# Input norm of each layer as plain transposes with the inverse roots multiplied in afterwards, and the last expert's products reordered around the combine

## The reference

```python
def layer(x):                                   # x: 512 x 1024
    h = x * rsqrt(mean(x * x, -1) + 1e-6) * norm1_g
    p = h @ w_in                                # 1024 -> 2304, split among three mixers
    x = x + concat(hgrn2(p), attention(p), s5(p)) @ w_out
    h = x * rsqrt(mean(x * x, -1) + 1e-6) * norm2_g
    # top 1 of 4 expert groups, top 2 of its 8 experts, for each token
    y_e = (silu(h_e @ w_gate[e]) * (h_e @ w_up[e])) @ w_down[e]     # 32 experts, FF 512
    return x + sum(gate[t, e] * y_e[t])
```

## Time and profile before

| | |
|---|---|
| three runs, median (lowest to highest) | 1594.12 us (1593.08 to 1594.84) |
| the profiled execution: its time, its span | 1589.54 us, 1587.6 us |
| PE busy, share of the span | 1534.9 us, 97% |
| DVE, ACT, POOL busy | 620.1, 428.6, 375.5 us |
| moved by transfers | 470.01 MB, 296 GB/s on average |
| opening of layer 0: PE's first group product | at 15.49 us |
| opening of layer 1: PE's first group product | at 801.70 us |
| PE's last product | starts 1577.4 us |

### The profile page before, as it was taken

How to read it: one execution, slowest core, us unless ns; L and a number is a source line. 1 busy time by engine, 2 the same in 40 slices (tenths; PEclk the granted TensorE clock), 3 DMA queues, 4 the chain that set the end, 5 groups by cost and what they waited for, 6 DMA issues and landing times.

```text
span 1587.6 us, 20334 instructions
## 1 busy us (share of the span) xinstructions
PE 1534.9 (97%) x8214; PEld 794.5 (50%) x8214; DVE 620.1 (39%) x1236; ACT 428.6 (27%) x766; POOL 375.5 (24%) x440
## 2 busy tenths in 40 slices
PE   8999999999999999998899999999999999999986
PEld 5655566555444444443357546655554444444432
DVE  1688546462122212311327965474622122123114
ACT  3664641211111111111235647403111111111102
POOL 5571880000000000000264637700000000000003
PEclk9999999999999999999999999999999999999999
DMA  9300403959999999999860003059699999999997
GB/s 394 144 0 14 146 2 85 419 219 420 429 427 426 428 426 427 428 426 427 339 272 1 0 28 134 1 165 417 236 426 427 425 427 427 426 427 428 425 427 297
DMA packets 57969, 470.01 MB, mean 296 GB/s; under 512 B 19417, under 2 KB 19545, under 8 KB 30194
## 3 DMA queue, kind: packets, MB, share of 16 engines
q1 hardware_dynamic: 50626, 452.37, 68.8%
q0 software_dynamic: 7104, 16.24, 2.8%
q10 hardware_dynamic: 144, 0.07, 0.0%
HBM read 447.69 MB, written 26.74 MB: 299 GB/s over the span
## 4 chain that ended last, share of the span: by engine, by line
PE 84%; DMA 11%; ACT 2%; DVE 2%; issue 1%; POOL 0%; POOLq 0%; SPq 0%; ACTq 0%; DVEq 0%
PE bank L1006 23%; PE bank L647 13%; PE bank L1043 11%; PE bank L996 9%; PE bank L778 7%; DMA hbuf<-wu 7%; DMA ring<-wd 4%; PE bank L641 2%; PE bank L709 2%; PE bank L722 2%; PE bank L739 2%; PE bank L983 1%; PE bank L1030 1%; PE bank L618 1%; PE bank L635 1%; PE bank L855 1%
## 5 line engine op out<-in xcount | busy, mean ns | idle before, releaser
L2225 POOL DMA_INDIRECT expert_rows<-raw_qd,store_rows x60 | 58.7, 979 | 1005.6 <-ACT raw_qd L1431 850.7
L1006 PE MATMUL bank<-ring,hbuf 128*64 128x512 f32 x640 | 281.2, 593 | 8.8 <-DMA ring<-wu 8.8
L1007 PE MATMUL bank<-ring,hbuf 128*64 128x512 f32 x640 | 281.5, 593 | 0.0
L1977 DVE COPY raw_qd<-bank 128x256 f32<-128x256 f32 x64 | 27.2, 425 | 642.5 <-PE bank L1030 642.5
L647 PE MATMUL bank<-hbuf,ring 128*128 128x512 f32 x480 | 210.0, 594 | 0.0
L1006 PEld LDWEIGHTS bank<-ring,hbuf 128*64 128x64 f32 x640 | 86.7, 137 | 187.1 <-issue 187.1
L1006 PE MATMUL bank<-raw_qd,hbuf 128*64 128x512 f32 x372 | 163.7, 592 | 3.4 <-DMA hbuf<-wu 3.4
L1043 PE MATMUL bank<-ring,raw_qd 128*64 128x512 f32 x352 | 160.4, 598 | 6.6 <-DMA ring<-wd 3.5
L1045 PE MATMUL bank<-ring,raw_qd 128*64 128x512 f32 x352 | 160.5, 598 | 0.0
L996 PE MATMUL bank<-raw_qd,x 128*128 128x192 f32 x896 | 159.5, 332 | 0.0
L1424 ACT ACTIVATE raw_qd<-bank 64x512 f32<-64x512 f32 x64 | 37.8, 591 | 418.6 <-PE bank L1007 418.6
(11 more groups left out here) (402 smaller groups left out, 2256.7 us busy)
## 6 DMA issues: line engine op xcount, KB each, us to landing
ring<-wd SPq DMA_DIRECT2D x40, 2048.0 KB, 21.4
ring<-wg SPq DMA_DIRECT2D x38, 2048.0 KB, 20.1
ring<-wu SPq DMA_DIRECT2D x34, 2048.0 KB, 23.3
ninth_slot<-wd SPq DMA_DIRECT2D x20, 2048.0 KB, 21.4
raw_qd<-wg SPq DMA_DIRECT2D x18, 2048.0 KB, 21.0
hbuf<-wu SPq DMA_DIRECT2D x18, 2048.0 KB, 23.5
ring<-w_in SPq DMA_DIRECT2D x8, 2048.0 KB, 18.3
raw_qd<-wg SPq DMA_DIRECT2D x6, 1792.0 KB, 13.3
```

The lines of the kernel that those rows point to most:

```text
L1006: mm(pb[2 + par][0:CAP, :], tokens[:, k, :], gates[k], start=(k == 0), stop=(k == KT - 1))
L1007: last = mm(pb[2 + par][CAP:P, :], tokens[:, k, :], ups[k], start=(k == 0), stop=(k == KT - 1))
L2225: G.indirect_dma_start(out=half_rows, out_offset=bass.IndirectOffsetOnAxis(ap=store_i[:, e:e + 1], axis=0), in_=y_sb[e % 2], in_offset=Non ...
```

## The change

Three edits.

**The opening.** PE turns x by plain transposes against the identity (L621 of the changed kernel), block by block as x arrives, for tiles 1 to 7. A product of the inverse roots, spread along a row, with the identity (`root_spread`, L627) puts the 512 roots along the tokens in every partition, into bank 0; ACT copies them out in two pieces (L1224: three blocks, then the last). Tile 0, whose bank held the roots, is turned after that. DVE alone copies the eight tiles out, with gain and roots multiplied in (L1533), tile 0 last. POOL's diagonals are gone. The products on the identity at the start are two, not seven.

**The first weights.** The first slot of `w_in` comes in halves, with the parameter pack between them; group 8 waits for the second half ahead of its fourth tile.

**The end.** The last down weights come in halves. The rows of expert 30 are combined for blocks 0 and 1 ahead of the last down products, and for block 2 right behind them; expert 31's rows follow once copied out (`late_rows`, L1105).

```diff
+        roots = hbuf[:, 4096:4096 + T]
+        TILES = (*range(1, KT), 0)
...
+        def first_weights(sp, layer):
+            sp.dma_start(ring[:, 0, 0:2048], w_in[layer, :, 0:2048]).then_inc(s_win[0], 16)
+            sp.dma_start(pk[:, :], pack[layer]).then_inc(s_pack, 16)
+            sp.dma_start(ring[:, 0, 2048:4096], w_in[layer, :, 2048:4096]).then_inc(s_out, 16)
...
-                if e == NE - 2:
-                    sp.dma_start(slot_tile[to][:, 0:half], wd[base + e, :, 0:half]).then_inc(s_down_half, 16)
+                if e >= NE - 2:
+                    first = s_down_half if e == NE - 2 else s_x[0]
+                    sp.dma_start(slot_tile[to][:, 0:half], wd[base + e, :, 0:half]).then_inc(first, 16)
...
             if layer == 0:
-                keep_running(7, 7, slice(0, P), ident)
+                keep_running(2, 7, slice(0, P), ident)
...
+            def root_spread(b):
+                pe.wait_ge(s_rstd, 2 * (NB * layer + b) + 2)
+                mm(pb[0][:, P * b:P * b + P], rstd[:, b:b + 1].broadcast_to([P, P]), ident,
+                   start=True, stop=True).then_inc(s["h"], 1)
+
+            for ready in range(NB):
+                x_ready(pe, layer, ready)
+                for b in range(ready + 1):
+                    for n in range(1, KT):
+                        if max(b, n // 2) == ready:
+                            turned_x(b, n)
+                if ready:
+                    root_spread(ready - 1)
+            pe.wait_ge(s["ev_a"], on("ev_a") + 1)
+            root_spread(NB - 1)
+            pe.wait_ge(s["ev_a"], on("ev_a") + 2)
             for b in range(NB):
-                pe.wait_ge(s["h"], on("h") + b + 1)
-                for n in range(KT):
-                    if layer > 0 and b == 0 and n % 2 == 0:
-                        x_ready(pe, layer, n // 2)
-                    last = mm(pb[n][:, P * b:P * b + P], x[:, b, P * n:P * n + P], scale_of[b], start=True, stop=True)
...
+                turned_x(b, 0)
...
+                if e == NE - 1:
+                    pe.wait_ge(s["cv"], 4)
+                    pe.wait_ge(s["ye"], NE - 1)
+                    for b in range(2):
+                        late_rows(b, 0, False)
                 down(e)
...
-            pe.wait_ge(s["cv"], 4)
+            pe.wait_ge(s["ht_e"], NE)
+            late_rows(2, 0, False)
             pe.wait_ge(s["ye"], NE)
-            for b in range(NB - 1):
-                combined(b, list(zip(selT, y_sb)))
...
+            for b in range(2):
+                late_rows(b, 1, True).then_inc(s["cb"], 1)
+            late_rows(2, 1, True).then_inc(s["cb"], 1)
...
-                pool.wait_ge(s_rstd, 2 * (NB * layer + b) + 2)
-                nc.gpsimd.tensor_scalar(scale_of[b], ident, rstd[:, b:b + 1], None, ALU.mult).then_inc(shared["h"], 1)
...
-            for n in range(1, KT, 2):
-                act.wait_ge(s["pe"], on("pe") + n + 1)
-                A(hT[:, n, :], pb[n][:, :], ACT.Copy, scale=pcol("norm1_g")[:, n:n + 1]).then_inc(s["ev_a"], 1)
+            for done, part in ((NB - 1, slice(0, P * (NB - 1))), (NB, slice(P * (NB - 1), T))):
+                act.wait_ge(s["h"], on("h") + done)
+                A(roots[:, part], pb[0][:, part], ACT.Copy).then_inc(s["ev_a"], 1)
...
-            for n in range(0, KT, 2):
-                dve.wait_ge(s["pe"], on("pe") + n + 1)
-                TS(hT[:, n, :], pb[n][:, :], pcol("norm1_g")[:, n:n + 1], None, ALU.mult).then_inc(s["ev_d"], 1)
+            dve.wait_ge(s["ev_a"], on("ev_a") + 2)
+            for done, n in enumerate(TILES):
+                dve.wait_ge(s["pe"], on("pe") + done + 1)
+                STT(out=hT[:, n, :], in0=pb[n][:, :], scalar=pcol("norm1_g")[:, n:n + 1], in1=roots,
+                    op0=ALU.mult, op1=ALU.mult).then_inc(s["ev_d"], 1)
```

More of the change, by code:

```diff
@@ L232, in trunk @@
         rel_late = small[:, 8:16]
-        scale_of = [hbuf[:, 7680 + P * i:7808 + P * i] for i in range(NB)]
+        roots = hbuf[:, 4096:4096 + T]
+        TILES = (*range(1, KT), 0)
         minus_half = small[:, 62:63]
@@ L258, in load_w_in @@
             sp.dma_start(ring[:, i, 0:width], w_in[layer, :, 4096 * i:4096 * i + width]).then_inc(s_win[i], 16)
+        def first_weights(sp, layer):
+            sp.dma_start(ring[:, 0, 0:2048], w_in[layer, :, 0:2048]).then_inc(s_win[0], 16)
+            sp.dma_start(pk[:, :], pack[layer]).then_inc(s_pack, 16)
+            sp.dma_start(ring[:, 0, 2048:4096], w_in[layer, :, 2048:4096]).then_inc(s_out, 16)
         names = dict(
-            s5p="S5 output parameters loaded", s5b="S5 input parameters loaded", h="Pool: diagonal of the inverse root mean squares of a block",
-            pe="PE: h^T and projection groups", ev_d="DVE: groups evacuated", ev_a="ACT: groups evacuated",
+            s5p="S5 output parameters loaded", s5b="S5 input parameters loaded", h="PE: inverse root mean squares of a block along its tokens, in every partition",
+            pe="PE: h^T and projection groups", ev_d="DVE: groups evacuated", ev_a="ACT: inverse roots of three blocks, of the last, then groups evacuated",
             dve="DVE: own chain", act="ACT: own chain", pool="Pool: own chain",
@@ L355, in by_vector @@
         def by_vector(n):
-            return n % 2 == 0 if n < KT else n < 13
+            return n < 13
         def wait_evacuated(engine, layer, n):
             s, on = of_layer(layer)
-            done = sum(by_vector(m) == by_vector(n) for m in range(n + 1))
+            done = sum(by_vector(m) == by_vector(n) for m in range(n + 1)) + (0 if by_vector(n) else 2)
             name = "ev_d" if by_vector(n) else "ev_a"
@@ L562, in sync_program @@
             if layer < L - 1:
-                sp.dma_start(pk[:, :], pack[layer + 1]).then_inc(s_pack, 16)
-                load_w_in(sp, layer + 1, 0)
+                first_weights(sp, layer + 1)
                 load_w_in(sp, layer + 1, 1)
@@ L627, in group @@
                 if c == 0:
[L628 removed]
+                    pe.wait_ge(s_win[i], 16 + 16 * layer)
                 if n >= KT + 4:
[L630 removed]
+                    wait_evacuated(pe, layer, n - 2 if n >= 18 else KT + 1 if n == KT + 4 else n - 4)
                 bank = group_bank(n)
@@ L643, in group @@
                 else:
-                    for k in range(KT):
+                    for i, k in enumerate(TILES):
                         if n == KT:
-                            wait_evacuated(pe, layer, k)
-                        last = mm(bank[:, :], w[:, k, c:c + P], hT[:, k, :], start=(k == 0), stop=(k == KT - 1))
+                            wait_evacuated(pe, layer, i)
+                            if k == KT // 2:
+                                pe.wait_ge(s_out, 16 * layer + 16)
+                        last = mm(bank[:, :], w[:, k, c:c + P], hT[:, k, :], start=(i == 0), stop=(i == KT - 1))
                 last.then_inc(s["pe"], 1)
@@ L1053, in down @@
                     pe.wait_ge(s["ye"], e - 1)
+                last_down = (slot[i], loaded(i, e, layer))
                 if e == NE - 2:
                     pe.wait_ge(s_down_half, 16 * (layer + 1))
-                pe.wait_ge(slot[i], loaded(i, e, layer))
-                down_of(e % 2, W_down[e % 3])
+                if e == NE - 1:
+                    pe.wait_ge(s_x[0], 16 * (layer + 2))
+                else:
+                    pe.wait_ge(*last_down)
+                down_of(e % 2, W_down[e % 3], loaded_last=last_down if e == NE - 1 else None)
             def weights_turned(i):
@@ L1071, in combined, with late_rows @@
                 last.then_inc(s["cb"], 1)
+            def late_rows(b, i, stop):
+                for half in range(2):
+                    r = slice(CAP * half, CAP * half + CAP)
+                    last = mm(pb[2 * b + half][:, :], selT[i][r, P * b:P * b + P], y_sb[i][r, :],
+                              start=(i == 0), stop=stop)
+                return last
             pick_block_by_block()
```

33 lines of the change are left out of this document (16 added, 17 removed).

## The result

| | before | after |
|---|---|---|
| median of the runs, us | 1594.12 (6 runs: 1589.87, then 1593.08 to 1594.84) | 1586.31 (6 runs); 1585.93 of the five at 1585.26 to 1586.93 (the sixth, 4038.71, was disturbed and is left out of the ratio) |
| ratio of the times | 1 | 0.9949, 95% interval 0.9937 to 0.9961 |
| profiled execution, its span | 1589.54, 1587.6 | 1585.26, 1583.4 |
| first group of layer 0, of layer 1 | 15.49, 801.70 | 13.31, 796.84 |
| DVE's last multiply starts | 1583.25 | 1579.09 |

The change makes the kernel faster by 0.51%, more than the 0.2% that can be told. The five runs' median lies 3.7 us under the forecast of 1589.6 and 2.1 under its range. The two profiled executions, however, differ by 4.28 us, where the sum said 4.55.

The account below looks back on a forecast made before the run. It took PE to bound the openings, and the weight stream, then PE, the layer's end; gains of 1.9 + 1.95 + 0.7 = 4.55 us off the 1594.12 us median gave 1589.6, range 1588.0 to 1597.0.

Parts of the forecast that it names:

- the sum: Whole kernel: 1.9 (opening, layer 0) + 1.95 (opening, layer 1) + 0.7 (end) = 4.55 us gained; bounds 0 to 4.75.
- Opening of layer 0: Start of layer 0: group 8 starts at 13.6 us instead of 15.49, a gain of 1.9 us.
- the prediction's own signs of being wrong: Group 8 at half rate, first multiply waiting for the pack, or group 8-to-combine stretch longer by the openings' gain; no size.
- The clock's rival: Both openings: transposes don't raise or keep up PE's clock, group 8 starts at half rate; 2.25 us slower, 1596.4; chance 0.2.
- Opening of layer 1: Start of layer 1: group 8 starts at 799.75 us instead of 801.70, a gain of 1.95 us.
- The end of layer 1: Last combine: DVE's last add no longer waits for PE, so the end comes 0.7 us earlier.
- The work behind the eight multiplies: Both layers, DVE's small work feeding POOL's chain: about 1.4 us later, costed at nothing; without cover up to 1.4 us a layer.

Follow-up runs that it names:

- forced: Kernel before, with DVE's two multiplies of the second head pair in layer 0 held until POOL reaches its wide products: 1594.84 us (12 runs).
- before with POOL held: Kernel before, with POOL's wide products held until DVE's two multiplies of the second head pair are done: 1589.43 us (12 runs).
- PE started early: Changed kernel with ACT's exponential for POOL moved ahead, and six PE products on zeros replacing the two on the identity: 1583.74 us (6 runs).
- The early start of POOL: Changed kernel with ACT's exponential that POOL waits for put ahead of the one that waits for DVE: 1583.14 us (6 runs), ratio to before 0.9944.
- The end alone: Kernel before with only the changed end of a layer, openings as before: 1589.83 us (12 runs), ratio 0.9983.

## Why the prediction was wrong

**The step that failed** is in the sum: "The runs' median lies 4.58 us above that execution, so I predict 1594.12 - 4.55". It takes the 4.58 us for a constant that the change leaves alone. The runs showed in its place the meeting of POOL and DVE at 180 us: forced, it is worth 5.4 us, the profiled execution of before doesn't have it (its two multiplies take 0.74 and 4.25 us), and by their times, for they have no profile, five of the six runs of before do. The changed kernel's five runs show none of it. Taken from the profiled execution alone the sum gives 1585.0, and the five runs have 1585.9. Where neither kernel has the meeting (before with POOL held, 1589.43, against 1586.23) the change's own steps are worth 3.2 us (medians on two chips), 1.4 less than reckoned. Holding POOL also spares the second multiply its wait, and the stretch to the first expert weights is 260.41 us there, 261.0 to 261.2 in ordinary executions of before; against those the change may be worth 0.6 to 0.8 more. The rest of the 8.2 us of the first comparison (1594.12 to 1585.93), and of the 5.6 on the second chip, I put down to the meeting, which in the changed kernel comes and goes with a fetch. The two numbers beside each other, 1589.54 and 1593 to 1595, said that the runs held something that the profile did not show; a rival in which the change does away with it was missing, and the range ended 3 us above the 1585.0 that it would have given.

**Opening of layer 0: right in the pair, and mis-sized as a constant.** Reckoned 13.6, found 13.31, a gain of 2.18 for 1.9; the multiply waits for the pack at 12.42, for 12.8. That wait is one of the prediction's own signs of being wrong, but its sum has the pack at 12.8 behind the roots at 12.6, so the sign contradicts the sum; the pack comes 0.17 us behind the roots here. In six other profiles with the new openings the first group starts at 13.68 to 14.95, and ACT's roots are last, as the rate of PE doubles only at 8.9 us or later; in the seventh, with PE started early, it is 13.23. With the old openings it was 14.96 to 16.45.

**The clock's rival is refuted.** Transposes with four spreads keep the full rate from 7.9 us to group 8, which runs at full rate from its first product (its two records in 1.10 us), and without the first products the rate rises too. The Trainium skill's rule on transposes (page "TensorE: Matmul & The Clock Gate", section "Part 4: PE-mode transpose") does not hold here: 13 take 1.58 us.

**Opening of layer 1: right in the pair.** Six us from block 3's products, reckoned 6, found 6.09. The six other profiles with both the new openings and the new end have 6.10 to 7.25, the ten with neither 7.22 to 7.52.

**The end of layer 1: as reckoned in the pair, and not shown beyond it.** From the issue of the first weights of expert 28 on SP (1470.70, then 1467.21) to DVE's last multiply (1583.25, 1579.09) are 112.55 and 111.88 us, 0.67 less for 0.7. As reckoned, the last add no longer waits for PE. But this stretch is 111.89 to 113.74 us in all eleven profiles with the old end and 110.97 to 114.07 in the eight with the new one, so the 0.67 is within what one execution differs from another.

**The work behind the eight multiplies was costed at nothing, and costs 0.6 and 1.4 us.** This is the second step that failed: the stretches to the first expert weights got longer by that much, 1.95 us in all. The prediction named the place, POOL's long chain, and the price, "up to 1.4 us a layer", if its cover is gone. The cover was there for the results, as it said; what was not seen is that DVE's instructions themselves take longer while POOL's run (1.92 and 1.07 us, for 1.22 and 0.17). The early start of POOL gives it back and more: 261.65 and 261.74 us fall to 260.45 and 260.54, and the runs by 3.1 (medians on two chips).

**What stays open.** The end alone had no long run in twelve, though its opening is that of before and its one profile has POOL 2.93 us ahead, as in the ordinary runs; no run here tells why. Nor is it told whether the end is worth more with the new openings (1.35 us by the medians) than with the old (some 0.7, against the runs of before under 1592.5). How the packet holds the store up no run here tells.

## What to carry to other kernels

When the profiled execution and the median differ by more than the runs of a level do, search for the second level first: take several profiles, cut them at the same issues, and the place shows in one stretch. Here DVE's multiply of two operands in SBUF took 3.8 to 4.3 us beside a 4 us product of POOL, and 0.74 otherwise, so where the two can meet, a wide POOL product is better ordered behind DVE's short ones by a semaphore than left to luck. A sum that agrees with one pair of profiles is to be compared stretch by stretch, since errors in it can cancel. Before a change is given the credit for a level that vanished, shift its code without changing its work.

## What the runs showed of the hardware

An instruction fetch beside a store of two times 256 KB goes with a later landing, and moving the code moved both: over 38 such stores in 19 profiles the next issue waited 2.70 to 2.73 us with no packet of the instruction queues beside it, 2.91 to 3.14 with one of q14 (8 KB), and 4.42 to 5.06 with one of q8 (16 KB), without exception.

PE's clock also falls now and then inside the late experts of layer 1, where PE waits for weights: to half, for some 3 us behind a wait of 1.94 to 2.23 us, in four of the eight profiles with the new end, and there in none of the eleven with the old one. In one execution of the changed kernel PE waited 2.23 us for the last but one down weights, and then (windows, columns as above):

```profile
1556.00:1559.00 3.00, 2.97 (x8) 0.51 0.88 310
...
1560.00:1561.00 1.00, 1.00 (x8) 1.00 0.97 373
```

In the opening the rise came anywhere from 7.9 to about 11.4 us when PE's first instruction started at 4.2 to 5.1, and by 6.3 when it started at 1.74.
